# Hybrid layers with a folded q norm, column groups and paired gated v products, and combine columns fetched during the experts stage

## The chip, the core and the metric

The kernel runs on one core of a Trainium2 chip. The metric is the device time of one execution of the whole program in microseconds (us). The core's engines run their own instruction streams and meet at semaphores: PE (TensorE, matrix products), DVE (VectorE), ACT (ScalarE), POOL (GpSimd) and SP (SyncE, which here only issues transfers).

## The reference

All is float32, on a sequence of 1024 tokens of width 1024. The first block is two hybrid layers, each a chunked gated delta rule (4 heads of 128) beside chunked gated linear attention (4 heads, keys of 64, values of 128):

```python
def l2norm(x):
    return x * lax.rsqrt(jnp.sum(x * x, axis=-1, keepdims=True) + 1e-6)
def head_rms_norm(o, g):
    return o * lax.rsqrt(jnp.mean(o * o, axis=-1, keepdims=True) + 1e-6) * g

def hybrid_layer(x, w_in, conv_w, ...):
    (dn_q, dn_k, dn_v, dn_z, dn_b, dn_a, g_q, g_k, g_v, g_z, g_r) = _split(x @ w_in, IN_SIZES)
    cq, ck, cv = silu(causal_short_conv([dn_q, dn_k, dn_v], conv_w))
    q = l2norm(cq) * (DN_DK ** -0.5);  k = l2norm(ck)
    beta = sigmoid(dn_b);  g = -exp(dn_a_log) * softplus(dn_a + dn_dt_bias)
    o_dn = gated_delta_rule_chunked(q, k, cv, g, beta)
    o_dn = head_rms_norm(o_dn, dn_norm_g) * silu(dn_z)
    log_f = log_sigmoid(g_r @ gla_gate_w2 + gla_gate_b) / 16
    o_gla = gla_chunked(g_q * (64 ** -0.5), g_k, g_v, log_f)
    o_gla = head_rms_norm(o_gla, gla_norm_g) * silu(g_z)
    return layer_norm(DEEPNORM_ALPHA * x + [o_dn, o_gla] @ w_out, ln_g, ln_b)
```

The second block is two more layers, each an attention (neighbourhood, then grouped query), a route of every token to 2 of 32 experts, the experts' gated products and a combine: each token gathers its two experts' rows, mixes them by its gates and is layer-normed, with an adaptive shift and scale (the second block's modulations, sums of a bias and of products with a weight) in the first of the two.

## The kernel before

The program is a row of stages, each with a stream for every engine: inputs, constants, then for each of the two layers `hybrid_stage` (line 334) and `out_stage` (1371); then the attention and route stages; `experts_stage` (2711) and `combine_stage` (2812), both twice. In the profiled run the first hybrid stage spans about 20 to 777 us, the second 862 to 1616, the first experts stage ends near 2957 and the first combine near 3028; the last combine is the end of the program, from 4332 on.

**Hybrid stage.** It begins with a small projection (805) of 80 columns of `w_in`: beta in rows 0 to 3, a in 32 to 35, r (the gate's rank 16) in 64 to 79. Its weights' place is cleared by POOL (1085), and the load waits for that. ACT and DVE then make g and beta from 4 rows of 1024 (1327 to 1338), which are stored to `g_dram` and read back as rows for each head.

Six jobs follow: DELTA jobs 0 to 3, one head each, and GATED jobs 4 and 5, a pair of heads each. A job has a prologue (projections of 128x512 pieces, `project` 493, their eviction, for a DELTA job a convolution, Silu, the norms' squares and sums by a product with ones, `sum_squares` 502, products kk and qk, 509, and transposes, 517) and a body (the inversion by levels, 672 and 695, w and u, 703 and 707, and the scan over 8 chunks, 715 to 723; for the pairs 754 to 784). PE interleaves by hand: while it runs a body it advances the next job's prologue, a generator, by a fixed number of steps at each gap; only the first prologue runs alone. What is left of the prologue runs at the end of the body, so the number of `yield`s in a prologue decides what stands at the boundary of two jobs. ACT, DVE and POOL do the same with labelled slots:

```python
GAPS = {DELTA: (4, 4, 1, 2), GATED: (5, 6, 2, 2), None: (0, 0, 0, 0)}
def advance(work, n):
    for _ in range(n):
        next(work, None)
```

The pieces of a prologue alternate between PSUM banks 6 and 7 in the order of `DELTA_PIECES` and `GATED_PIECES`; a piece waits until the piece before it in its bank has been read.

At a job's end ACT copies the last half of o (983), squares o (985), evicts z1 (846) and copies x (955); PE then starts the next levels (672), and behind the first of them sums o's squares (`norm_sums` 647). Behind DELTA job 3 the order is another: the sums come at once, and DVE's exponent and evictions of the gated pair (1170, 1265) behind them. The root of a norm is ACT's (943 to 945). For q and k, ACT takes Ln and Exp of the sums (877, 879), and DVE multiplies (1131 for k, 1134 for q, where the factor 128 ** -0.5 goes in).

Beside the pairs' bodies, and behind the last, the six modulation vectors' sums are made (`sum_mod`, 594 to 608): for each vector two column groups, a product with the bias (604) and one with ones (608), then an ACT copy and a store (915, 917).

**Combine.** SP loads four column vectors (ln_g, ln_b, shift, scale) in a pattern whose runs are single 4-byte elements (2833), waits, then loads the next stage's weights; POOL gathers rows (2851); DVE waits for the columns, scales them (2971) and then mixes (2937). The last combine has no such columns. In the experts stage SP loads each expert's weights (2735), PE multiplies them (2634, tiles of 128x32 with 256 columns), and POOL gathers the tokens (2769).

## Time and profile before

| quantity | value |
|---|---|
| median of 3 runs | 4391.09 us (4390.46 to 4391.94) |
| profiled execution, its own time | 4389.45 us |
| its span | 4387.6 us |
| mean granted TensorE clock | 0.953 |
| PE busy | 3937.8 us, 90% |
| DVE busy | 2126.6 us, 48% |
| ACT busy | 1036.6 us, 24% |
| POOL busy | 626.0 us, 14% |

The profile is one execution. A time in a row is in us from the span's start. A float32 product is recorded as two passes, so a count of matmuls is twice that of the code. Idle time ahead of an instruction stands in brackets, with what ended it ("issue" when the profile shows no releaser). The granted clock is a share of full speed, 2.4 GHz; the lower level, 1.2 GHz, is 0.50. Idle time of an engine that is not the last to arrive costs nothing.

### The profile page before, as it was taken

The page shows a single profiled execution, that of the slowest core. Times are in us where ns is not written, and L with a number is a line of the kernel's source. Part 1 is how long each engine was busy: PE and PEld are TensorE (multiplying, and loading weights), DVE is VectorE, ACT ScalarE, POOL GpSimd, SP SyncE. Part 2 cuts the span into 40 slices and gives each one's busy share as a digit, 9 for nine tenths or more (in the row PEclk, how much of TensorE's full clock was granted, in tenths as well). Part 3 has the DMA queues.
Part 4 walks back from the last instruction along what each step waited for, and adds up shares of the span by engine and source line. Part 5 has one row for each costly group of instructions (what it writes and reads, how often), then busy time and mean ns, then how long its engine had stood idle before and what let it go on. Part 6 is the DMA issues. An engine that isn't in the chain of part 4 may idle for free. (4 is left out here: it accounts for less than half of the span.)

```text
span 4387.6 us, 79942 instructions
## 1 busy us (share of the span) xinstructions
PE 3937.8 (90%) x34826; PEld 2430.8 (55%) x34826; DVE 2126.6 (48%) x3076; ACT 1036.6 (24%) x1779; POOL 626.0 (14%) x462
## 2 busy tenths in 40 slices
PE   7999999899999998999996999875999999699973
PEld 3555655445556644666544666543566665466642
DVE  4555365455554555555565222215566787422214
ACT  3333223134432221222210000003444540000002
POOL 1232011022310110000000211101221300111111
PEclk9999999999999999999997999987999999799996
DMA  3232202323331225454522999983000112699997
GB/s 106 100 113 92 72 30 82 83 83 105 103 101 30 92 71 160 77 87 72 98 97 102 393 421 410 418 360 106 15 1 15 39 57 85 235 420 418 409 422 275
DMA packets 259927, 707.72 MB, mean 161 GB/s; under 512 B 59195, under 2 KB 185091, under 8 KB 234103
## 3 DMA queue, kind: packets, MB, share of 16 engines
q1 hardware_dynamic: 245127, 657.91, 42.2%
q0 software_dynamic: 13248, 40.38, 2.5%
q8 instruction: 280, 4.59, 0.4%
q10 hardware_dynamic: 1200, 4.24, 0.3%
q14 instruction: 72, 0.59, 0.0%
HBM read 630.25 MB, written 63.82 MB: 158 GB/s over the span
## 5 line engine op out<-in xcount | busy, mean ns | idle before, releaser
L2677 DVE TENSOR_TENSOR sb_work<-sb_work,ps 128x384 f32<-128x384 f32 (+2 forms) x66 | 34.2, 519 | 715.4 <-ACT sb_work L2664 715.4
L493 PE MATMUL ps<-sb_mixT,sb_work 128*128 128x512 f32 x768 | 359.4, 604 | 9.6 <-ACT sb_x_tok L846 5.5
L493 PE MATMUL ps<-sb_xT,sb_work 128*128 128x512 f32 x768 | 357.5, 602 | 9.6 <-ACT sb_x_tok L846 5.5
L2664 ACT ACTIVATE sb_work<-ps 128x384 f32<-128x384 f32 (+2 forms) x66 | 30.4, 461 | 1047.3 <-PE ps L2634 1047.3
L1634 PE MATMUL ps<-sb_xT,sb_work 128*128 128x512 f32 x512 | 236.2, 599 | 0.0
L2634 PE MATMUL ps<-sb_work,sb_mixT 128*32 128x256 f32 x3264 | 192.0, 398 | 41.9 <-DMA sb_work<-moe_w_up 32.4
L2634 PE MATMUL ps<-sb_work,sb_xT 128*32 128x256 f32 x3264 | 190.4, 395 | 39.7 <-DMA sb_work<-moe_w_up 30.1
L493 PEld LDWEIGHTS ps<-sb_mixT,sb_work 128*128 128x128 f32 x768 | 138.0, 192 | 147.8 <-issue 129.9
L493 PEld LDWEIGHTS ps<-sb_xT,sb_work 128*128 128x128 f32 x768 | 137.4, 191 | 147.0 <-issue 129.1
L2121 DVE TENSOR_REDUCE sb_cols<-ps 128x1 f32<-128x1024 f32 x128 | 150.7, 1219 | 85.6 <-PE ps L1964 85.5
L2634 PEld LDWEIGHTS ps<-sb_work,sb_mixT 128*32 128x32 f32 x3264 | 126.9, 115 | 106.5 <-issue 49.7
L2634 PEld LDWEIGHTS ps<-sb_work,sb_xT 128*32 128x32 f32 x3264 | 125.5, 114 | 103.9 <-issue 46.0
L2634 PE MATMUL ps<-sb_mixT,sb_xT 128*32 128x256 f32 x2496 | 146.0, 395 | 25.6 <-DMA sb_mixT<-moe_w_up 25.6
L2634 PE MATMUL ps<-sb_xT,sb_mixT 128*32 128x256 f32 x2496 | 143.8, 391 | 22.6 <-DMA sb_xT<-moe_w_up 22.6
L1940 PE MATMUL ps<-sb_work,sb_mixT 128*128 128x384 f32 x448 | 154.5, 491 | 4.1 <-PEq L93 4.1
L1634 PEld LDWEIGHTS ps<-sb_xT,sb_work 128*128 128x128 f32 x512 | 91.0, 190 | 104.2 <-issue 104.2
L2045 ACT ACTIVATE sb_work<-ps,sb_cols 128x1024 f32<-128x1024 f32 x128 | 142.7, 1115 | 17.6 <-DVE sb_cols L2121 12.1
L1974 PEld LDWEIGHTS ps<-sb_const,sb_work 128*128 128x128 f32 x1024 | 110.3, 141 | 63.3 <-issue 32.9
L1974 PE MATMUL ps<-sb_const,sb_work 128*128 128x128 f32 x1024 | 141.8, 281 | 1.9 <-DVE sb_work L2129 0.9
L2769 POOL DMA_INDIRECT sb_xT<-scratch_h,sb_slots x87 | 84.6, 973 | 400.8 <-DVE sb_xT L2672 379.5
L2769 POOL DMA_INDIRECT sb_mixT<-scratch_h,sb_slots x87 | 84.6, 972 | 400.5 <-DVE sb_mixT L2672 379.5
L2647 PE MATMUL ps<-sb_work 128*32 128x256 f32 x2496 | 141.3, 379 | 0.0
(486 smaller groups left out, 7276.1 us busy)
## 6 DMA issues: line engine op xcount, KB each, us to landing
sb_work<-moe_w_gate SPq DMA_DIRECT2D x34, 2048.0 KB, 15.2
sb_work<-moe_w_up SPq DMA_DIRECT2D x34, 2048.0 KB, 19.7
sb_work<-moe_w_down SPq DMA_DIRECT2D x32, 2048.0 KB, 22.0
sb_mixT<-moe_w_down SPq DMA_DIRECT2D x17, 2048.0 KB
sb_xT<-moe_w_down SPq DMA_DIRECT2D x17, 2048.0 KB
sb_xT<-moe_w_gate SPq DMA_DIRECT2D x16, 2048.0 KB, 16.9
sb_xT<-moe_w_up SPq DMA_DIRECT2D x16, 2048.0 KB, 21.5
sb_mixT<-moe_w_gate SPq DMA_DIRECT2D x16, 2048.0 KB, 17.1
```

Source lines behind the costliest of these rows:

```text
L493: last = pe.matmul(m.ps[:, bank, :], b.w[i][:, k, :], m.xT[:, k, half * HALF:(half + 1) * HALF], start=(k == 0), stop=(k == NK - 1))
L1634: last = pe.matmul(m.ps[:, bank, :], w[j // 2][:, k, :], m.xT[:, k, j % 2 * HALF:(j % 2 + 1) * HALF], start=(k == 0), stop=(k == NK - 1))
L1940: last = pe.matmul(m.ps[:, bank, 0:WIDE], m.xT[:, k, n * P:(n + 1) * P], w[:, k, :], start=(k == 0), stop=(k == NK - 1))
L1974: last = pe.transpose(m.ps[:, 4 + half, b * P:(b + 1) * P], prob[i % 2][head][:, half * HALF + b * P:half * HALF + (b + 1) * P], ident(m))
L2045: act.activation(prob[i % 2][head], banks(m, 2 * head), ACT.Exp, bias=top[:, column(i, head)], accum_out=total[:, column(i, head)]).then_i ...
L2121: dve.tensor_reduce(top[:, column(i, head)], banks(m, 2 * head), AX.X, ALU.max, negate=True).then_inc(found, 1)
L2634: last = pe.matmul(strip_sums(2 + 2 * (n % 2), tile[j])[:, g, :], b.x_turned[n % 2][:, g, k, :], b.gate_up[n % 2][:, :, k, j * P:(j + 1) * ...
L2647: last = pe.matmul(strip_sums(y_bank(n), tile[j])[:, g, :], b.act_turned[n % 2][:, g, k, :], b.down[n % 2][:, k, j * 2 * P:(j + 1) * 2 * P ...
L2664: act.activation(b.act[n % 2][:, 0:strips[n], :], strip_sums(2 + 2 * (n % 2))[:, 0:strips[n], 0:P], ACT.Silu).then_inc(silued, 1)
L2677: dve.tensor_tensor(act, act, strip_sums(2 + 2 * (n % 2))[:, 0:strips[n], P:2 * P], ALU.mult).then_inc(multiplied, 1)
L2769: pool.indirect_dma_start(b.x[n % 2][:, g, :], None, token_quarters(m), bass.IndirectOffsetOnAxis(m.slots[:, g, at:at + 1], 0)).then_inc(g ...
```

## The change

- **Small projection.** The sequence is cut into four quarters of 256, each the output of one column group: a tile of 32 columns of weights (r in rows 0 to 15, then beta and a, twice, from `ROW_BETA` on), four of them side by side in one bank. The operations on rows work on 256 columns at the rows of all groups. The memset goes; a_log and dt_bias come in eight small loads issued by ACT; r is copied in four pieces and g stored in four.
- **q norm folded.** The norm of o divides out a factor of q, so q is no longer normed: q's sums, roots and multiplication go. What is left of it is the epsilon: ACT squares q with scale 0.128 (in the middle of the body), DVE adds that to o's squares (`finish_squares`, at the start of the next body), and PE's norm sums wait for the addition. DVE's slots move up, and the prologue has 26 steps for 28.
- **Paired v.** The gated v projections of a pair take 256 columns of weights at once, in four pieces v0 to v3 of two token tiles each.
- **Modulation sums.** `sum_mods` makes two vectors at once in four column groups, three times; one copy and one store each.
- **Combine columns.** Their four loads move to the start of the experts stage, to a place of their own (`cols2`); the combine stage's waits for them go, and its first load is the next stage's weights.

```diff
-                ("sum_k0", 7), ("sum_k1", 7), ("sum_q0", 7), ("sum_q1", 7), ("kk0", 7), ("kk1", 7),
+                ("sum_k0", 7), ("sum_k1", 7), ("kk0", 7), ("kk1", 7),
                 ("v_tok0", 7), ("v_tok1", 7), ("k_tok0", 7), ("k_tok1", 7), ("qk0", 7), ("qk1", 7))
 GATED_PIECES = (("gate0", 6), ("gate1", 7), ("k0", 6), ("k1", 7), ("q0", 6), ("q1", 7), ("zA0", 6), ("zA1", 7),
-                ("zB0", 6), ("zB1", 7), ("vA0", 6), ("vA1", 7), ("vB0", 6), ("vB1", 7))
+                ("zB0", 6), ("zB1", 7), ("v0", 6), ("v1", 7), ("v2", 6), ("v3", 7))
...
-    b.root_k, b.root_q = b.raw[0], b.raw[1]
+    b.root_k, b.q_square = b.raw[0], m.spare[:, D:2 * D]
...
+    b.g_v_pair = m.x_tok[:, 6:8, :], m.work[:, 16 * SEQ:18 * SEQ].rearrange("p (h n) -> p h n", h=2)
+    b.w_v = m.work[:, 7 * SEQ:11 * SEQ].rearrange("p (h k n) -> p h k n", h=2, n=P)[:, :, 0:NK, :]
...
-DVE_SLOTS = {DELTA: {3: "k", 5: "q", "u": "v", "b1": "norm_k", "a2": "norm_q", "a3": "kk0", "a4": "kk1", "b4": "v_tok0",
-                     "a5": "v_tok1", "a6": "k_tok0", "b6": "k_tok1", "a7": "qk0", "end": "qk1"},
+DVE_SLOTS = {DELTA: {3: "k", 5: "q", "u": "v", "b1": "norm_k", "a2": "decay_q", "b2": "kk0", "a3": "kk1", "a4": "v_tok0",
+                     "b4": "v_tok1", "a5": "k_tok0", "a6": "k_tok1", "b6": "qk0", "a7": "qk1"},
...
-            sp.wait_ge(cleared, 1)
-            for at, column, n in ((0, C_BETA, 4), (32, C_A, 4), (64, C_GR, RANK)):
+            for at, column, n in ((0, C_GR, RANK), (ROW_BETA, C_BETA, 8), (ROW_BETA + 8, C_BETA, 8)):
...
+            sp.wait_ge(act_small, 2)
+            for j in range(4):
+                sp.dma_start(m.rows[64:64 + RANK, j * QUARTER:(j + 1) * QUARTER], b.r_rows[32 * j:32 * j + RANK, :]).then_inc(
+                    rows_stored, 16)
             sp.wait_ge(dve_small, 3)
-            sp.dma_start(g_dram[0:4, :], m.rows[32:36, :]).then_inc(rows_stored, 16)
-            sp.dma_start(g_dram[4:8, :], m.rows[0:4, :]).then_inc(rows_stored, 16)
-            sp.wait_ge(rows_stored, 32)
+            for j in range(4):
+                sp.dma_start(g_dram[:, j * QUARTER:(j + 1) * QUARTER], b.rows[32 * j + ROW_BETA:32 * j + ROW_A + DN_HEADS, :]).then_inc(
+                    rows_stored, 16)
+            sp.wait_ge(rows_stored, 128)
             load_rows(0)
...
-                sum_squares(job, "k", b.root_k, 0, 2 * job + 1)
+                sum_squares(job, "k", b.root_k, 0, job + 1)
                 yield
                 next(gate)
                 yield
-                sum_squares(job, "k", b.root_k, 1, 2 * job + 1)
+                sum_squares(job, "k", b.root_k, 1, job + 1)
                 yield
-                next(gate)
-                yield
-                sum_squares(job, "q", b.root_q, 0, 2 * job + 2)
-                yield
-                next(gate)
-                yield
-                sum_squares(job, "q", b.root_q, 1, 2 * job + 2)
-                yield
-                for _ in range(5):
+                for _ in range(7):
...
-                for i, name in ((4, "vA"), (5, "vB")):
-                    for half in range(2):
-                        bank = take_bank(job, f"{name}{half}")
-                        if half == 0:
+                for n in range(4):
+                    bank = take_bank(job, f"v{n}")
+                    if n == 0:
+                        for i in (4, 5):
                             pe.wait_ge(w_loaded[i], 16 * (pair + 1))
-                        for n in range(4 * NK):
-                            t, k = half * 4 + n // NK, n % NK
-                            last = pe.matmul(m.ps[:, bank, n // NK * P:(n // NK + 1) * P], m.xT[:, k, t * P:(t + 1) * P],
-                                             b.w[i][:, k, :], start=(k == 0), stop=(k == NK - 1))
-                            if n == 4 * NK - 1:
+                    for t in (2 * n, 2 * n + 1):
+                        for k in range(NK):
+                            last = pe.matmul(m.ps[:, bank, t % 2 * 2 * P:(t % 2 + 1) * 2 * P], m.xT[:, k, t * P:(t + 1) * P],
+                                             b.w_v[:, :, k, :], start=(k == 0), stop=(k == NK - 1))
+                            if t % 2 == 1 and k == NK - 1:
                                 last.then_inc(filled[bank], 1)
-                            if n % 4 == 3:
+                            if k % 2 == 1:
                                 yield
...
+                def sum_mods(pair):
+                    bank = 6 + pair % 2
+                    outs = [m.ps[32 * n:32 * n + 1, bank, :] for n in range(4)]
+                    if pair < 2:
+                        wait_freed(pe, len(JOBS) - 1, f"v{2 + pair}")
                     else:
-                        pe.wait_ge(part_copied, 2 * len(part_of) - 5 + v)
-                    for half in range(2):
-                        pe.matmul(outs[half], ident(m, N_MODS)[:, v:v + 1], halves(b.mod_bias)[half],
+                        pe.wait_ge(part_copied, 2 * len(part_of) - 1)
+                    for n in range(4):
+                        pe.matmul(outs[n], ident(m, N_MODS)[:, 2 * pair + n // 2:2 * pair + n // 2 + 1], halves(b.mod_bias)[n % 2],
                                   start=True, stop=False)
-                    pe.wait_ge(w_loaded[v], 16 * ((len(JOBS) if v < 4 else GLA_HEADS // 2) + 1))
-                    for half in range(2):
-                        last = pe.matmul(outs[half], ones(m)[:, 0:1], halves(b.mod_w[v])[half], start=False, stop=True)
+                    for v in (2 * pair, 2 * pair + 1):
+                        pe.wait_ge(w_loaded[v], 16 * ((len(JOBS) if v < 4 else GLA_HEADS // 2) + 1))
+                    for n in range(4):
+                        last = pe.matmul(outs[n], ones(m)[:, 0:1], halves(b.mod_w[2 * pair + n // 2])[n % 2], start=False, stop=True)
                     last.then_inc(mod_summed, 1)
...
-            for half in range(2):
-                for k in range(NK):
-                    last = pe.matmul(m.ps[0:80, half, :], b.small_w[:, k, :], m.xT[:, k, half * HALF:(half + 1) * HALF],
-                                     start=(k == 0), stop=(k == NK - 1))
+            for k in range(NK):
+                for j in range(4):
+                    last = pe.matmul(m.ps[32 * j:32 * j + 32, 0, 0:QUARTER], b.small_w[:, k, :],
+                                     m.xT[:, k, j * QUARTER:(j + 1) * QUARTER], start=(k == 0), stop=(k == NK - 1))
...
-                for n, (x, r) in enumerate(((b.kT, b.root_k), (b.qT, b.root_q))):
-                    act.wait_ge(silued, 3 * j + n + 1)
-                    act.activation(r, x, ACT.Square).then_inc(squared, 1)
+                act.wait_ge(silued, 3 * j + 1)
+                act.activation(b.root_k, b.kT, ACT.Square).then_inc(squared, 1)
...
-                for n, (name, r) in enumerate((("sum_k", b.root_k), ("sum_q", b.root_q))):
-                    for half in range(2):
-                        src, free = wait_filled(act, j, f"{name}{half}")
-                        act.activation(halves(r)[half], src, ACT.Ln, bias=m.eps6[:]).then_inc(free, 1)
-                    wait_freed(act, j, f"{name}1")
-                    act.activation(r, r, ACT.Exp, scale=-0.5).then_inc(rooted, 1)
+                for half in range(2):
+                    src, free = wait_filled(act, j, f"sum_k{half}")
+                    act.activation(halves(b.root_k)[half], src, ACT.Ln, bias=m.eps6[:]).then_inc(free, 1)
+                wait_freed(act, j, "sum_k1")
+                act.activation(b.root_k, b.root_k, ACT.Exp, scale=-0.5).then_inc(rooted, 1)
...
+                    if n == 2:
+                        if j:
+                            act.wait_ge(o_squared, norms_before[j])
+                        act.activation(b.q_square, b.qT, ACT.Square, scale=1e-3 * DN_DK).then_inc(q_squared, 1)
...
-                act.activation(b.root, b.oT, ACT.Square).then_inc(o_squared, 1)
+                act.activation(b.root, b.oT, ACT.Square).then_inc(o_half_squared, 1)
...
+            for j in range(4):
+                at = slice(32 * j + ROW_A, 32 * j + ROW_A + DN_HEADS)
+                act.dma_start(m.dt_bias[at, :], a["dn_dt_bias"][l].unsqueeze(1)).then_inc(a_loaded, 16)
+                act.dma_start(m.a_log[at, :], a["dn_a_log"][l].unsqueeze(1)).then_inc(a_loaded, 16)
...
-                dve.wait_ge(rooted, 2 * j + 1)
+                dve.wait_ge(rooted, j + 1)
                 dve.tensor_tensor(b.kT, b.kT, b.root_k, ALU.mult).then_inc(normed, 1)
                 yield "norm_k"
-                dve.wait_ge(rooted, 2 * j + 2)
-                dve.scalar_tensor_tensor(b.qT, b.qT, DN_DK ** -0.5, b.root_q, ALU.mult, ALU.mult).then_inc(normed, 1)
-                dve.wait_ge(normed, 2 * j + 2)
+                dve.wait_ge(silued, 3 * j + 2)
                 dve.wait_ge(decayed, 3 * (j + 1))
                 dve.tensor_tensor(b.qg[par], b.qT, b.G_row, ALU.mult)
-                yield "norm_q"
+                yield "decay_q"
...
+            def finish_squares(job):
+
+                if job < DN_HEADS:
+                    dve.wait_ge(q_squared, job + 1)
+                    dve.wait_ge(o_half_squared, job + 1)
+                    dve.tensor_tensor(b.root, b.root, b.q_square, ALU.add).then_inc(o_squared, 1)
...
+                if j:
+                    finish_squares(j - 1)
...
+                finish_squares(j - 1)
...
-            pool.memset(b.small_w, 0.0).then_inc(cleared, 1)
...
+            for n, src in enumerate(columns):
+                sp.dma_start(m.cols2[:, 8 * n:8 * n + 8], src.rearrange("(k p) -> p k", p=P),
+                             allow_slow_non_contiguous=True).then_inc(s["loaded_e"], 16)
...
-            if columns is not None:
-                for dst, src in zip((ln_g, ln_b, shift, scale), columns):
-                    sp.dma_start(dst, src.rearrange("(k p) -> p k", p=P), allow_slow_non_contiguous=True).then_inc(
-                        columns_loaded, 16)
+            if out is None:
                 load_group_weights(sp, first_weights, group_buffers(m).w, 0, first_loaded)
-                sp.wait_ge(columns_loaded, 64)
...
-            if columns is not None:
-                dve.wait_ge(columns_loaded, 64)
+            if out is None:
```

## Rows read from the trace of the kernel before

**Rows 1.** The page's first part: busy us, share of the span, instructions of each engine.
```profile
PE 3937.8 (90%) x34826; PEld 2430.8 (55%) x34826; DVE 2126.6 (48%) x3076; ACT 1036.6 (24%) x1779; POOL 626.0 (14%) x462
```
**Rows 2.** Windows: from:to, us, busy us (instructions) by engine, granted clock, DMA share, GB/s.
```profile
165.00:265.00 100.00, 94.97 (x653) 56.70 (x653) 59.28 (x65) 41.19 (x55) 29.98 (x14) 1.00 0.28 94
687.00:698.00 11.00, 10.80 (x49) 3.84 (x50) 9.50 (x11) 2.83 (x5) 4.72 (x2) 0.53 0.54 219
2412.00:2430.00 18.00, 18.00 (x340) 10.04 (x336) 5.38 (x6) 0.49 (x1) 7.34 (x8) 1.00 0.73 266
```
**Rows 3.** Timeline: start, duration, engine, line, out<-in, count, [idle before <-releaser]; layer 0, small projection.
```profile
30.36 13.93 PE L805 MATMUL ps<-sb_xT,sb_work 128*80 128x512 f32 x32 [0.72 <-DVE sb_xT L1322]
44.22 0.26 PE L809 MATMUL ps<-sb_const,sb_work 52*128 52x52 f32 x1
```
**Rows 4.** The same view, layer 1, small projection.
```profile
862.35 0.63 POOL L1085 MEMSET sb_work<- 128x640 f32 x1 [134.82 <-POOLq L93]
867.07 16.11 PE L805 MATMUL ps<-sb_mixT,sb_work 128*80 128x512 f32 x32 [6.47 <-DMA sb_work<-w_in]
```
**Rows 5.** The same view, a piece of the first experts stage.
```profile
2419.56 10.53 PE L2634 MATMUL ps<-sb_xT,sb_mixT 128*32 128x256 f32 x192
```
**Rows 6.** The same view, the first delta head's prologue, layer 0.
```profile
91.40 1.13 PE L502 MATMUL ps<-sb_x_tok,sb_const 128*128 128x512 f32 x2
100.56 1.13 PE L493 MATMUL ps<-sb_xT,sb_work 128*128 128x512 f32 x2 [0.95 <-ACT sb_work L846]
```
**Rows 7.** The same view, inside head 0's body, layer 0.
```profile
181.84 1.12 PE L502 MATMUL ps<-sb_x_tok,sb_const 128*128 128x512 f32 x2 [1.21 <-ACT sb_x_tok L846]
186.52 0.28 DVE L1243 TENSOR_TENSOR sb_work<-sb_work,ps 128x128 f32<-128x128 f32 x1
```
**Rows 8.** The same view, from head 0 to head 1.
```profile
214.27 1.06 ACT L985 ACTIVATE sb_mixT<-sb_mixT 128x1024 f32<-128x1024 f32 x1
216.28 1.01 ACT L955 COPY sb_work<-ps 128x1024 f32<-128x1024 f32 x1 [0.28 <-PE ps L655]
217.39 1.15 PE L672 MATMUL ps<-sb_work 64*64 64x64 f32 x32 [1.15 <-issue]
```
**Rows 9.** The same view, from head 3 to the first gated pair.
```profile
547.36 1.06 ACT L985 ACTIVATE sb_mixT<-sb_mixT 128x1024 f32<-128x1024 f32 x1
548.47 1.98 PE L647 MATMUL ps<-sb_mixT,sb_const 128*128 128x512 f32 x4
552.64 1.61 DVE L1170 TENSOR_SCALAR sb_x_tok<-ps,sb_conv 128x512 f32<-128x512 f32 x2 [1.19 <-PE ps L573]
```
**Rows 10.** The same view, the gated pairs' v projections.
```profile
540.07 1.95 PE L586 MATMUL ps<-sb_work,sb_xT 128*128 128x128 f32 x16
633.40 3.74 PE L586 MATMUL ps<-sb_work,sb_xT 128*128 128x128 f32 x32
```
**Rows 11.** The same view, the gated pairs' bodies and the end of the stage.
```profile
575.09 1.98 PE L493 MATMUL ps<-sb_xT,sb_work 128*128 128x512 f32 x4 [2.49 <-ACT sb_work L846]
687.20 1.87 PE L604 MATMUL ps<-sb_rows,sb_const 6*1 6x512 f32 x4 [2.76 <-ACT sb_work L915]
696.52 1.35 DVE L1280 COPY_PREDICATED sb_work<-sb_const,ps 128x512 f32<-128x512 int32 x2 [1.45 <-PE ps L754]
757.38 1.02 PE L604 MATMUL ps<-sb_rows,sb_const 6*1 6x512 f32 x4
758.33 1.03 PE L608 MATMUL ps<-sb_work,sb_const 128*1 128x512 f32 x4
```
**Rows 12.** The same view, the first combine, then the last.
```profile
2958.58 0.94 POOL L2851 DMA_INDIRECT sb_work<-scratch_y,sb_dest  x1 [70.86 <-issue]
2974.65 0.17 DVE L2971 TENSOR_SCALAR sb_cols<-sb_cols 128x8 f32<-128x8 f32 x1 [21.93 <-DMA sb_cols<-scratch_mods]
4332.93 0.94 POOL L2851 DMA_INDIRECT sb_work<-scratch_y,sb_dest  x1 [71.80 <-issue]
4339.49 1.28 DVE L2937 SCALAR_TENSOR_TENSOR sb_x_tok<-sb_work,sb_gates,sb_x_tok 128x1024 f32<-128x1024 f32 x1 [12.22 <-DMA sb_work<-scratch_y,sb_dest]
```

199 lines of the change are left out of this document (105 added, 94 removed).

## The prediction, made before the changed kernel was timed

> **What bounds the kernel now.** I read the page's busy line first: TensorE is busy 3937.8 of 4387.6 us, the next engine (VectorE) 2126.6 [rows 1]. The share is a mean over stages, so I then read the windows. In a typical 100 us of a hybrid layer, across one whole head's body, PE is busy 94.97 us at full clock, VectorE 59.28, ScalarE 41.19, and DMA moves at 0.28 of its rate [rows 2]. So in the hybrid stage a pass taken from PE is time taken from the program, except where PE isn't the last to arrive. Those places I looked up in the timeline, one for each edit; they decide how much of the removed work comes back. The end of the first experts stage is different: there VectorE and PE both stand still for a transfer [rows 12].
>
> The sum is made against the profiled execution, whose span is 4387.6 us; its own time is 4389.45, and the median of the runs shown is 4391.09, 3.5 above the span.
>
> **A. Small projection, columns in groups.** Now 32 recorded passes of 512 columns (each f32 product is recorded as two) run from 30.36 until the next instruction at 44.22: 13.86 us [rows 3], 0.43 a pass. The change has 64 passes of a 128x32 tile with 256 columns, four tiles side by side. The nearest row is the experts' product with just this shape: 192 in 10.53 us, 0.0548 each [rows 5]. 64 x 0.0548 = 3.5, with a fixed end of 0.2 it is 3.7, so layer 0 gains 10.1. In layer 1 the block takes 16.11 against 13.93, 2.2 more for the same work: it starts after 6.47 us of idle PE [rows 4], and I put the 2.2 down to half clock at its start. The new one pays the same 2.2: 5.9, gain 10.1. The memset of 0.63 us ahead of the small weights' load goes, and with it its wait: 0.7 in layer 1, where the block waits for that very load [rows 4]; layer 0 has its transposes to do and gains nothing. The row operations that follow (on a quarter of the columns each) were hidden behind the first projections and stay so, with more room; the eight tiny loads of constants by ScalarE and the twelve small copies and stores that replace three sit there too, and the first to need the rows is a body some 60 us later. I cost them at nothing and, should a queue hold them up, at a few us. A: 20.9, bounds 0 (a pass of 256 columns would cost half of 0.43, 64 x 0.215 = 13.8) to 22.
>
> **B. The q norm folded, first head.** The q norm's sums are two blocks of two passes; in the first prologue nothing but PE's own work runs, so their 0.96 each (1.13 less the tail) [rows 6] come back whole: 1.9. The wait of 0.95 for the z eviction by ScalarE [rows 6] was ScalarE's Ln, Ln, Exp for q ahead of it: they go, 0.95. With a small rest, 3.0 a layer, 6.0. Bounds 2 and 7.
>
> **C. The q norm folded, heads 1 to 3.** Here the prologue runs between the steps of the previous head's body. PE loses 4 passes, 1.72 us, a head. The wait of 1.21 us ahead of the sums [rows 7] goes too, but what follows in that step waits for VectorE, whose convolution keeps it until 186.52, where it makes the new values [rows 7]: PE comes earlier and waits. The other half of the argument is the head's boundary. Two steps of the generator less means that the last two pieces (1.76 us of PE work) are no longer there to fill the boundary. Its start is set by ScalarE: Square of o at 214.27 for 1.06, z's eviction, the copy of x at 216.28 for 1.01, after which PE begins the levels at 217.39, having been idle for 1.15 [rows 8]. Earlier work on PE doesn't move this chain, which hangs on the last o of the scan. VectorE's new addition (q's square onto o's) is hidden: o's square is ready at 215.33, the addition of some 1.28 (the nearest row is the 128x1024 step in [rows 12]) would be done at 216.6, and nobody needs it before PE's norm sums, behind the levels that start at 217.39. ScalarE's Square of q, 1.06, goes into the middle of the body, where ScalarE is 41% busy [rows 2]. So of 1.72 + 1.21 a head I count 0.6, the part that neither VectorE nor the boundary takes back: 3.6 for six heads. Bounds 0 (all is given back) and 10.3 (6 x 1.72, all is kept).
>
> **D. The q norm folded, from head 3 to the pair.** Between the last delta head and the first gated pair the norm sums follow at once: Square of o at 547.36 for 1.06, PE's sums at 548.47 [rows 9]. Now the addition stands between them: 1.28 and a semaphore, PE 1.3 later. VectorE itself is taken: the exponent and the gated k's eviction at 552.64 [rows 9] come later by as much and a bit more, say 1.7 in all. What is queued behind the addition on VectorE is just this exponent, and the levels of the pair wait for it. Cost 1.7 a layer, 3.4. Bounds 0 and 5.
>
> **E. Paired v products.** 16 passes with 128 columns take 1.95 us and 32 take 3.74 [rows 10]: (3.74 - 1.95) / 16 = 0.112 each. A layer has two jobs of 128 products in two passes, 512 passes, 57.2 us. 256 passes of 256 columns, at half of 0.43, are 55.0. Gain 2.1 a layer, 4.2. With 4 x 0.0548 = 0.219 a pass it is 1.1 a layer; if the loads of 128-column weights hid worse than they do now it could be 3. That v's weights 4 and 5 are now both wanted at v0 costs nothing: they are loaded a job ahead. Bounds 1 and 6.
>
> **F. Modulation sums in four groups.** The last sums show four passes in 0.95 us (757.38 to 758.33), two beside each other [rows 11]; the last pair has 16, 3.8 us. Four beside each other halve it: 1.9 a layer, on the path, since nothing else is left for PE. The earlier ones lie in the pair's bodies, where PE waits 2.76 us for ScalarE's store of the sums ahead of 687.20 and VectorE is idle for 1.45 at 696.52 [rows 11]. Three evictions for six take a part of that wait: I count 1.2 a layer. 6.2 together. Bounds 3.8 and 11.4 (all passes halved, 5.7 a layer).
>
> **G. The combine's columns.** In the first combine VectorE scales the columns at 2974.65, after 21.93 us of waiting for their landing; the first gather was issued at 2958.58. In the last combine, without columns, it is issued at 4332.93 and the first mix starts at 4339.49, 6.56 later [rows 12]. So without the column wait the first mix could start at 2965.2; it now follows the scaling, 2975.2. That is 10. But in the first combine the next stage's weights load beside the gathers, so I take 7.5. Bounds 2.5 and 10. The loads now stand at the start of the experts stage on SyncE's queue, behind which the experts' weights wait. From 2412 to 2430 PE is busy for 18.00 of 18.00 us at a DMA share of 0.73 [rows 2], so there is room of nearly 5 us; I count nothing. If they aren't covered they cost up to 5.
> The trace shows these loads to be dear: four of 4 KB end 16 us after the gathers start. The Trainium skill, DMA: Bandwidth & Descriptors, Rules for kernel authors, says that a strided last dimension is lowered to one descriptor per element, which by its word is the case for each of them; by that rule the cost moves with them into the experts stage, and G would be at its lower end, 2.5 instead of 7.5, and the sum 40.
>
> **Sum.** 20.9 + 6.0 + 3.6 - 3.4 + 4.2 + 6.2 + 7.5 = 45.0. Span 4387.6 - 45.0 = 4342.6; the median 4391.1 - 45.0 = 4346.1.
>
> **Rivals.** 1: *All removed PE work counts.* 20.9 + 4 x 4 passes x 0.43 x 2 layers (13.8) + 2.4 for the waits of the first head + 4.2 + 11.4 + 7.5 = 60.2: 4331. For it: PE's 95% [rows 2]. Against it: ScalarE's chain at the boundary [rows 8] and D. 0.17.
> 2: *The clock falls at the boundaries.* With the fill gone, PE's idle time there grows from 1.15 to some 2.7 us. After 2.76 us idle at 687.20 four passes took 1.87 us, against 1.02 at 757.38, and the granted clock from 687 to 698 was 0.53: the lower level, 1.2 GHz [rows 2, 11]. After 2.49 us at 575.09 four 512-column passes took 1.98, which is full clock [rows 11]. So it is near the edge. A fall costs up to 0.47 x 11 = 5.2 us; part of what follows waits for other engines, so I take 2 at each of six boundaries, 12: 4358. 0.15.
> The Trainium skill, TensorE: Matmul & The Clock Gate, HAM oscillation, says that idle stretches between groups of matmuls throttle the engine again each time; the row at 687.20 agrees and the one at 575.09 doesn't show it.
> 3: *The combine is bound by its gathers,* or the moved loads cost what they give: G is 0, 4353. 0.07.
> 4: *Column groups don't run side by side at this place.* A and F's halving are nothing: 4346 + 20 + 6 = 4372. Against it are 192 passes at 0.0548 [rows 5]. 0.03.
> 5: *Slower.* The half clock of rival 2, held: after each of the eight boundaries (four a layer, the one of part D included) PE stays at 1.2 GHz. It decides from the point where it eats 45 us and 8.8 more, 6.7 a boundary, that is 13.5 us at half clock after each. The only stretch like it is the 11 us at 0.53 [rows 2]. 0.01.
>
> **Chances and range.** Forecast 0.57, rivals 0.17, 0.15, 0.07, 0.03, 0.01. The forecast's own range, from the bounds of C, F and G, is 4338 to 4354. To hold 8 in 10 it must reach nearly to rivals 1 and 2: 4331 to 4358. A measurement of this kernel can tell about 0.2%, 8.8 us, from no change. All cases but the last lie beyond it on the fast side; for mishaps I have not thought of I add a little: faster 0.96, same 0.02, slower 0.02.
>
> **What the new profile should show.** A: the small product's block of some 3.7 us in layer 0, under 6 in layer 1. B, C: the ones-product only for k, half as many; PE's idle time ahead of the levels up from 1.15. D: the sums of head 3 released by VectorE, some 1.3 later after Square. E: the v block of 64 at about 0.22 a pass. F: three groups of sums. G: the first combine's VectorE starting some 7 to 9 us after the first gather; the experts' first products without a new DMA wait. The windows' clock behind each boundary settles rival 2. What would make it wrong above all: C near one of its ends, or the moved column loads holding up the experts' weights.

## The result, and the profile after

The changed kernel took 4350.28 us (median of 4, 4349.7 to 4351.16) beside 4390.83 us for the kernel before (4390.46 to 4391.94): a ratio of 0.991, 95% interval 0.9898 to 0.9923, 40.5 us less. The forecast was 4346.1, 45.0 less; the range was 4331 to 4358. The profiled execution has a span of 4349.0 us for 4387.6, 38.6 less, and a mean clock of 0.951 for 0.953. The busy line of the page answers to [rows 1]:

```profile
PE 3894.6 (90%) x34318; PEld 2403.2 (55%) x34318; DVE 2108.5 (48%) x3081; ACT 1007.0 (23%) x1749; POOL 624.2 (14%) x460
```

PE is busy for 43.2 us less, with 508 passes fewer, and its share is again 90%.

The sum over the parts can be checked, since most instructions have a counterpart in both kernels. I took the start of the same instruction in both timelines, and how much earlier it is in the changed kernel. The same marks, taken on a second trace of the unedited changed kernel (after_again, below), differ by -0.7 us at the first and -1.1 at the end of the second hybrid stage, so a difference between two marks is good to some 0.4 us there, but for one thing that is told below (the clock).

| mark | before | after | earlier by |
|---|---|---|---|
| layer 0, small projection done | 44.22 | 34.85 | 9.4 |
| head 0's levels begin | 114.12 | 100.88 | 13.2 |
| norm sums of head 0, behind the first levels of head 1 | 218.47 | 205.17 | 13.3 |
| w of head 1 | 279.66 | 267.40 | 12.3 |
| norm sums of head 1 | 321.23 | 308.35 | 12.9 |
| norm sums of head 2 | 423.99 | 410.48 | 13.5 |
| w of head 3 | 504.10 | 491.25 | 12.9 |
| norm sums of head 3 | 548.47 | 536.05 | 12.4 |
| levels of the last pair | 675.18 | 661.81 | 13.4 |
| its scan | 736.54 | 722.22 | 14.3 |
| output stage | 777.44 | 762.50 | 14.9 |
| layer 1, small projection done | 883.11 | 857.03 | 26.1 |
| head 0's levels begin | 952.99 | 923.07 | 29.9 |
| w of head 3 | 1343.38 | 1313.68 | 29.7 |
| norm sums of head 3 | 1387.75 | 1358.48 | 29.3 |
| levels of the last pair | 1516.02 | 1485.83 | 30.2 |
| output stage | 1617.52 | 1586.96 | 30.6 |
| first gather of the first combine | 2958.58 | 2928.07 | 30.5 |
| its first mix | 2975.22 | 2937.95 | 37.3 |
| last combine, first mix | 4339.49 | 4301.55 | 37.9 |

Term by term, with the letters of the prediction:

| term | forecast | found | by |
|---|---|---|---|
| A, small projection | 20.9 | 20.5 | marks: 9.4, and 26.1 - 14.9 |
| B, fold, first head | 6.0 | 7.7 | marks |
| C, fold, heads 1 to 3 | 3.6 | -0.6 | marks |
| D, fold, head 3 to the pair | -3.4 | -2.6 | undo_fold |
| E, paired v | 4.2 | 3.7 | undo_pairs |
| F, modulation sums | 6.2 | 2.0 | marks |
| G, combine's columns | 7.5 | 6.8 | marks of this pair of traces |
| the rest | 0 | 1.2 | |
| all | 45.0 | 38.7 | the spans' 38.6 |

**A.** The timeline of PE, the rows that answer to [rows 3] and [rows 4] (start, duration, engine, line, out<-in, count, idle before):

```profile
31.26 3.66 PE L815 MATMUL ps<-sb_xT,sb_work 128*32 128x256 f32 x64 [0.72 <-DVE sb_xT L1351]
34.85 0.26 PE L819 MATMUL ps<-sb_const,sb_work 52*128 52x52 f32 x1
```
```profile
851.16 5.94 PE L815 MATMUL ps<-sb_mixT,sb_work 128*32 128x256 f32 x64 [5.61 <-DMA sb_work<-w_in]
857.03 0.26 PE L819 MATMUL ps<-sb_const,sb_work 52*128 52x52 f32 x1
```

The block takes 3.59 and 5.87 us until the next instruction, against 13.86 and 16.04. 64 passes with 256 columns in four groups run 0.056 apart, what the experts' row [rows 5] had given. In layer 1 the block starts behind a wait for the weights at half clock (the granted clock from 851.2 to 857.0 is 0.60), which costs 2.3 us, as it cost 2.2 before.

**C.** Waits of PE from 0 to 1640 us (engine, tile and line, what released it: us in all, times, longest us); the line of the levels is 672 before and 682 after. Before:

```profile
PE ps L672 <- issue: 6.9, 6, 1.1
PE ps L672 <- ACT sb_work L955: 2.4, 2, 1.2
...
PE ps L754 <- issue: 6.6, 5, 2.0
PE ps L754 <- DVE sb_work L1280: 2.3, 2, 1.1
```

After:

```profile
PE ps L682 <- ACT sb_work L966: 16.3, 8, 2.3
PE ps L657 <- DVE sb_mixT L1226: 1.4, 1, 1.4
...
PE ps L764 <- issue: 13.6, 10, 2.0
PE ps L764 <- DVE sb_work L1308: 6.0, 2, 3.0
PE ps L764 <- POOL sb_work L1125: 2.9, 1, 2.9
PE ps L834 <- issue: 2.4, 2, 1.2
```

The wait ahead of a body's levels was 9.3 us in eight and is 16.3: 2.3 at each of the six boundaries of two heads, where it was 1.15 (the two first heads keep their 1.2). Of the 10.3 us of q sums' passes that are gone, 7.0 came back as idle time of PE at these boundaries. Behind the first of these waits the clock was lower:

```profile
203.53 1.71 PE L682 MATMUL ps<-sb_work 64*64 64x64 f32 x32 [2.33 <-ACT sb_work L966]
205.17 3.02 PE L657 MATMUL ps<-sb_mixT,sb_const 128*128 128x512 f32 x4
```
```profile
200.00:207.00 7.00, 4.67 (x45) 3.35 (x44) 3.70 (x3) 4.19 (x6) 2.87 (x3) 0.78 0.70 228
```

The norm sums take 3.02 us; before, at full clock, they took 1.98 (as in [rows 9]). The windows' columns are those of [rows 2]: the granted clock is 0.78 in these 7 us, so a part of them ran at 1.2 GHz. From the norm sums to w of head 1, 1.0 us is lost in layer 0 and 1.4 in layer 1; a part of the fall lies ahead of the norm sums (1.71 us for the levels' products, which take 1.15 at full clock), and a trace without it, undo_combine_2 below, puts the whole at 1.6 in each layer. Behind the other four boundaries of two heads, with the same idle time, the granted clock is 1.00.

**F.** In the last pair's levels PE waits at 764 for VectorE and GpSimd (and "issue"), 22.5 us in the two layers where it was 8.9, with 5.5 more for the sums' evictions. The window of the levels, 671.60 to 736.50 before and 658.30 to 722.20 after:

```profile
671.60:736.50 64.90, 58.16 (x356) 28.41 (x355) 57.60 (x61) 23.21 (x26) 17.42 (x7) 0.89 0.31 122
```
```profile
658.30:722.20 63.90, 51.56 (x355) 27.97 (x353) 58.59 (x61) 22.06 (x24) 17.43 (x7) 0.92 0.34 133
```

PE has 6.6 us less to do, the window is 1.0 shorter, and VectorE is busy for 58.6 of 63.9 us: by its busy share this stretch is VectorE's. No run made VectorE faster here; that less work of PE is worth nothing in it is what undo_sums shows.

### The profile page after: what moved, and what is told of

Same layout as the page of the kernel before. It is cut to its first block and busy times, and to the rows that moved or that the text cites. A ratio compares the mean times of both kernels' runs of the same rounds, so it can differ in the third digit from the quotient of the medians.

```text
span 4349.0 us, 78912 instructions
## 1 busy us (share of the span) xinstructions
PE 3894.6 (90%) x34318; PEld 2403.2 (55%) x34318; DVE 2108.5 (48%) x3081; ACT 1007.0 (23%) x1749; POOL 624.2 (14%) x460
## 5 line engine op out<-in xcount | busy, mean ns | idle before, releaser
L2075 ACT ACTIVATE sb_work<-ps,sb_cols 128x1024 f32<-128x1024 f32 x128 | 142.6, 1114 | 17.8 <-DVE sb_cols L2151 12.3
## 6 DMA issues: line engine op xcount, KB each, us to landing
sb_work<-moe_w_gate SPq DMA_DIRECT2D x34, 2048.0 KB, 14.3
```

The lines of the kernel that those rows point to most:

```text
L2075: act.activation(prob[i % 2][head], banks(m, 2 * head), ACT.Exp, bias=top[:, column(i, head)], accum_out=total[:, column(i, head)]).then_i ...
```

## The experiments

In the five comparisons the kernel before took 4390.8, 4402.9, 4385.9, 4397.3 and 4388.8 us, and the traces part by up to 8 us in the first experts stage alone (551.9 to 559.7 us from its first gather of tokens to the combine's first gather), where the DMA share is 0.98. So an edit of the hybrid stages is read by the marks (within a trace, from the first mark on), and whole times are compared only between kernels of one comparison.

### Undoing one part of the change

**undo_fold**: q normed as before (its two sums, two Ln, Exp, Square, multiplication, VectorE's slots, 28 steps), `finish_squares` gone.

```diff
-                for _ in range(7):
+                next(gate)
+                yield
+                sum_squares(job, "q", b.root_q, 0, 2 * job + 2)
+                yield
+                next(gate)
+                yield
+                sum_squares(job, "q", b.root_q, 1, 2 * job + 2)
+                yield
+                for _ in range(5):
                     next(gate)
                     yield
...
-                    dve.wait_ge(o_half_squared, job + 1)
-                    dve.tensor_tensor(b.root, b.root, b.q_square, ALU.add).then_inc(o_squared, 1)
```

> The changed kernel with q normed as before: its sums, roots and multiplication back, the Square of q and the addition gone, VectorE's slots and the 28 steps as before. Theory, from the marks of both traces: the first head's prologue is worth 7.7 us, heads 1 to 3 are worth -0.6 (the passes saved are idle time at the boundaries, less the fall of the clock after the first and the late copies in head 3's levels), the boundary of head 3 costs 2.8; together 4.3: 4354.6. Rival (the prediction's terms B, C, D): 6.2, 4356.5.

Measured: 4370.2 us, ratio 0.993 (0.9913 to 0.9946). Marks, as differences from the changed kernel: the first prologue costs 3.4 us more in each layer; from there to the norm sums of head 2 it is 0.3 more in layer 0 and 0.2 in layer 1, made of 1.9 in each for the passes, less 1.6 in each for the clock (the size of that fall is taken from undo_combine_2 below); from w of head 3 to its norm sums 1.3 less in each layer. So the fold is worth 6.7 (B), 0.5 (C) and -2.6 (D), 4.6 in all. By the marks the sum at the end of layer 1 is 5.4, with a step of 1.8 in the first pair of layer 0 that isn't the fold's (see the clock below). The theory stands; the prediction's B was right, its C was not, since it left the clock out.

**undo_sums**: one modulation vector at a time, two column groups, six evictions.

```diff
-                def sum_mods(pair):
+                def sum_mod(v):
...
-                for pause, pair in ((5, 0), (3, 1)):
-                    sum_mods(pair)
-                    yield
+                for pause, first in ((4, 0), (2, 2)):
+                    for v in (first, first + 1):
+                        sum_mod(v)
+                        yield
```

> The changed kernel with the modulation sums made one vector at a time in two column groups, as before. Theory: in the levels of the last pair VectorE sets the pace, so only the last sums' share counts, 2.0 us by the differences of the two traces at the stage's marks: 4352.3. Rival (the prediction's term): 6.2 us, 4356.5.

Measured: 4362.39 us, ratio 0.9914 (0.9897 to 0.993). Marks: in the last pair's levels 0.0 in layer 0 and -0.5 in layer 1, in its scan +0.6 in both. So four of the six sums are worth nothing, and the last two 0.6 a layer, a third of the 1.9 of PE's time that they save.

**undo_pairs**: v in four pieces of 128-column products.

```diff
-                            last = pe.matmul(m.ps[:, bank, t % 2 * 2 * P:(t % 2 + 1) * 2 * P], m.xT[:, k, t * P:(t + 1) * P],
-                                             b.w_v[:, :, k, :], start=(k == 0), stop=(k == NK - 1))
+                            last = pe.matmul(m.ps[:, bank, n // NK * P:(n // NK + 1) * P], m.xT[:, k, t * P:(t + 1) * P],
+                                             b.w[i][:, k, :], start=(k == 0), stop=(k == NK - 1))
```

> The changed kernel with the v products of 128 columns, four pieces per pair of heads. Theory: 0.95 us a job from the scan's steps (3.67 to 3.55 us a step), four jobs, 3.8: 4354.1. Rival: in the first pair's jobs it is swallowed by the boundary of head 3, so only half: 4352.2.

Measured: 4366.53 us, ratio 0.9924 (0.9907 to 0.994). Marks: 0.90, 0.94, 0.90 and 0.93 us in the four jobs, 3.7. A step of the pair's scan in the changed kernel, which answers to [rows 10]:

```profile
620.98 3.62 PE L599 MATMUL ps<-sb_work,sb_xT 128*128 128x256 f32 x16
624.53 0.44 PE L785 MATMUL ps<-sb_x_tok,sb_v_tok 128*64 128x128 f32 x4
```

16 passes of 256 columns in 3.55 us to the next instruction, 0.222 each, where 32 of 128 had taken 3.67.

### The combine's columns

**undo_combine** (and **undo_combine_2**, the same code again): the four column loads back in the combine stage; **only_combine**: the kernel before with the move alone; **after_again**: the changed kernel unedited.

```diff
+            if columns is not None:
+                for dst, src in zip((ln_g, ln_b, shift, scale), columns):
+                    sp.dma_start(dst, src.rearrange("(k p) -> p k", p=P), allow_slow_non_contiguous=True).then_inc(
+                        columns_loaded, 16)
                 load_group_weights(sp, first_weights, group_buffers(m).w, 0, first_loaded)
...
-            for n, src in enumerate(columns):
-                sp.dma_start(m.cols2[:, 8 * n:8 * n + 8], src.rearrange("(k p) -> p k", p=P),
```

> The changed kernel with the four column loads back in the combine stage, waits and order of the weights' load included. Theory: the trace of the changed kernel has the first mix 6.8 us closer to the stage's start, and this is kept to the end: 4350.3 + 6.8 = 4357.1. Rival: the moved loads hold up the experts' weights and give a part back, so that undoing them costs less, 4 us or under: 4354.

Measured: 4362.25 us, ratio 0.9917 (0.99 to 0.9934), the same as undo_sums in the same comparison. Its trace, and the changed kernel's:

```profile
2931.46 0.94 POOL L2881 DMA_INDIRECT sb_work<-scratch_y,sb_dest  x1 [70.22 <-issue]
2941.12 0.17 DVE L3001 TENSOR_SCALAR sb_cols<-sb_cols 128x8 f32<-128x8 f32 x1 [15.56 <-DMA sb_cols<-scratch_mods]
2941.69 1.28 DVE L2967 SCALAR_TENSOR_TENSOR sb_x_tok<-sb_work,sb_gates,sb_x_tok 128x1024 f32<-128x1024 f32 x1
```
```profile
2928.07 0.94 POOL L2879 DMA_INDIRECT sb_work<-scratch_y,sb_dest  x1 [69.12 <-issue]
2937.95 1.28 DVE L2965 SCALAR_TENSOR_TENSOR sb_x_tok<-sb_work,sb_gates,sb_x_tok 128x1024 f32<-128x1024 f32 x1 [9.83 <-DMA sb_work<-scratch_y,sb_dest]
```

The first mix starts 10.23 us behind the first gather with the column loads, and 9.88 us without them; in the kernel before it was 16.64 [rows 12]. That called for the next three.

> The changed kernel itself, unedited, on the chip of the next two, for a base of their times and for the stretch from the first gather to the first mix. Theory (the prediction's): 9.9 us there again. Ratio to the kernel before 0.991 again.

> The same kernel as undo_combine, again, since its trace had the first mix 10.2 us behind the first gather, where the kernel before has 16.6. Theory 1: the column loads cost about 6.8 us when they stand in the combine stage, and undo_combine's trace was a lucky one: 4 to 7 us slower than after_again. Theory 2: they land before the gathered rows anyway, the gathers set the first mix, and the 16.6 us of the kernel before were that trace's own: within 2 us of after_again.

> The kernel before with the move of the four column loads alone. Theory 1: 7 us faster than the kernel before. Theory 2: within 2 us of it.

Measured, in one comparison: before 4385.86 us, only_combine 4384.04 (ratio 0.9993, 0.9984 to 1.0002), after_again 4349.35 (0.9914, 0.99 to 0.9927), undo_combine_2 4350.27 (0.9921, 0.9907 to 0.9935). The move is worth 1.8 us in the kernel before and 0.9 in the changed one, by medians; neither is clear of the scatter, and the trace of undo_combine_2 is 0.9 ahead of after_again's at the end of the second hybrid stage, where their code is the same. From first gather to first mix: 9.9 in only_combine, 9.7 in after_again, 10.4 in undo_combine_2:

```profile
2924.21 0.94 POOL L2881 DMA_INDIRECT sb_work<-scratch_y,sb_dest  x1 [70.69 <-issue]
2934.03 0.17 DVE L3001 TENSOR_SCALAR sb_cols<-sb_cols 128x8 f32<-128x8 f32 x1 [15.71 <-DMA sb_cols<-scratch_mods]
2934.60 1.28 DVE L2967 SCALAR_TENSOR_TENSOR sb_x_tok<-sb_work,sb_gates,sb_x_tok 128x1024 f32<-128x1024 f32 x1
```

The single executions say more. The 15 of the kernel before lie in two groups, eight at 4380.4 to 4385.9 and seven at 4389.8 to 4393.0. The 11 of only_combine all lie at 4380.7 to 4385.7. undo_combine_2 has four at 4347.3 to 4352.0 and one at 4358.0, undo_combine three at 4361.1 to 4362.7 and one at 4368.6. A reading that fits is that the column loads cost nearly nothing in about half of the executions and some 7 us in the others, and that the move takes those away. The execution profiled before (4389.45) shows the late landing, those of undo_combine and undo_combine_2 the early one, and they lie in the lower part of their comparisons. But it is not shown: a trace of the kernel before from the lower group was not taken, and times can part as widely without these loads in the combine (fill, which has moved them, lies at 4349.97 to 4364.76). What decides how late they land is open.

### The boundary of two heads, and the clock

**fill**: two empty steps where the q sums stood, VectorE's slots as before the change.

```diff
-                for _ in range(7):
+                for _ in range(2):
                     next(gate)
                     yield
+                    yield
+                for _ in range(5):
+                    next(gate)
+                    yield
```

> The changed kernel with two empty steps in the prologue of a delta head where the q sums' steps were (28 again, VectorE's slots as before). So two pieces of projection stand at the boundary of two heads again. Theory: PE's idle time ahead of the levels falls from 2.3 to about 1.15 us at the six boundaries between heads, the clock doesn't fall behind the first of each layer (2.5 us), and the scan with its last o ends earlier by the 1.7 us that the pieces take: 1.2 to 1.7 a boundary and 2.5, together 10 to 12 us by the marks of the hybrid stages. Rival: in the steps left empty PE waits for VectorE's new values, and nothing but the clock's 2.5 us comes back.

Measured: 4357.76 us, ratio 0.9911 (0.9895 to 0.9928). The wait ahead of the levels (686 here) is what it was before the change, 6.9 and 2.4 in all:

```profile
PE ps L537 <- DVE sb_work L1181: 9.2, 8, 1.4
PE ps L686 <- issue: 6.9, 6, 1.1
PE ps L537 <- DVE sb_work L1167: 4.6, 6, 0.8
PE ps L529 <- DVE sb_work L1181: 4.4, 8, 0.6
PE ps L735 <- DVE sb_work L1275: 4.1, 6, 0.7
PE ps L686 <- ACT sb_work L970: 2.4, 2, 1.2
```

Marks from the changed kernel's: 1.0 and 1.4 us come back between the norm sums of head 0 and w of head 1, where the clock stays at 1.00 now; at the boundaries themselves 0.8, 0.3 and 0.2 us in layer 0, 0.5, 0.3 and 0.2 in layer 1, 2.3 together. The first of each layer holds the early part of the fall, 0.6 and 0.2, so the clock is worth 3.2 and the six boundaries some 0.25 each, 1.5. Together 4.7, not 10 to 12. The rival of this experiment is nearer. In the scan, PE's waits for VectorE at 529, 537 and 735 are 22.3 us, where the changed kernel has 14.7 (at 529 and 537, and none of 735's kind): with two steps empty PE waits there for VectorE's new values and pieces, and the filled boundary has mostly moved the wait. What the q sums cost in the scan shows against undo_fold, which has the same boundary and the same slots of VectorE: from w of head 0 to w of head 1, and from there to w of head 2, fill is 0.9 us shorter each time in both layers. So taking a head's q sums out, 1.72 us of passes, is worth half of its time where the boundary stays filled, and some 0.6 us a head in the changed kernel, where it doesn't.

**halved**: Square of o and the addition in two halves, the first in the middle of the scan.

```diff
+                        act.wait_ge(o_copied, 2 * j + c // 4 + 1)
+                        act.activation(halves(b.root)[c // 4], halves(b.oT)[c // 4], ACT.Square).then_inc(o_half_squared, 1)
-                act.wait_ge(o_copied, 2 * (j + 1))
-                act.activation(b.root, b.oT, ACT.Square).then_inc(o_half_squared, 1)
...
+                    if c == 5:
+                        dve.wait_ge(q_squared, j + 1)
+                        dve.wait_ge(o_half_squared, 2 * j + 1)
+                        dve.tensor_tensor(halves(b.root)[0], halves(b.root)[0], halves(b.q_square)[0], ALU.add)
```

> The changed kernel with ScalarE's Square of o and VectorE's addition each done in two halves, the first half in the middle of the scan, as soon as the first half of o is copied. Theory: ScalarE's chain at each boundary of two heads is 0.5 us shorter (six times, 3), and from head 3 to the pair the wait of PE's sums for the addition is 1.1 us shorter (twice, 2.2): 5 us by the marks. Rival: the chain isn't ScalarE's, but hangs on the last o alone: under 1.

Measured: 4358.8 us, ratio 0.9915 (0.9899 to 0.9932). Marks: from w of head 3 to its norm sums 1.03 us less in each layer, the theory's 1.1; the wait for the addition is 0.3 (it was 1.4). The wait ahead of the levels is 13.8 us in eight, at most 1.9, for 16.3 and 2.3:

```profile
PE ps L682 <- ACT sb_work L966: 13.8, 8, 1.9
PE ps L657 <- DVE sb_mixT L1225: 0.3, 1, 0.3
```
```profile
202.76 1.43 PE L682 MATMUL ps<-sb_work 64*64 64x64 f32 x32 [1.90 <-ACT sb_work L966]
204.11 3.34 PE L657 MATMUL ps<-sb_mixT,sb_const 128*128 128x512 f32 x4
```

So ScalarE's chain does set the boundary, by 0.4 us each. But behind 1.90 us of idle time the clock fell too, at three of the six boundaries: at the first of layer 0 the norm sums take 3.34.

**square_early**: the Square of q behind the norm's roots, a level earlier.

```diff
-                    if n == 2:
-                        if j:
-                            act.wait_ge(o_squared, norms_before[j])
-                        act.activation(b.q_square, b.qT, ACT.Square, scale=1e-3 * DN_DK).then_inc(q_squared, 1)
...
+                    if n == 1:
+                        if j:
+                            act.wait_ge(o_squared, norms_before[j])
+                        act.activation(b.q_square, b.qT, ACT.Square, scale=1e-3 * DN_DK).then_inc(q_squared, 1)
```

> The changed kernel with ScalarE's Square of q right behind the norm's roots instead of ahead of the second level's copies. Theory: in head 3's levels, where k's eviction stands just ahead of it, the Square made the copies late: 0.66 us in layer 0 and 0.45 in layer 1 come back, 1.1; nothing in heads 1 and 2. Rival: the loss there has another source: 0.

Measured: 4357.5 us, ratio 0.991 (0.9893 to 0.9926). From the norm sums of head 2 to w of head 3 it is 0.2 us shorter than the changed kernel's, and so is after_again, which has no edit. My theory of the late copies falls; the Square of q costs nothing in either place. What the marks had shown in head 3's levels (0.7 and 0.5 us) is of the size by which that stretch differs between kernels that are equal in it (-0.2 in undo_pairs, 0.5 in fill, 0.9 in halved). It holds a wait of 5.5 us for ScalarE, in all kernels, behind which PE runs at a lower clock for a while (0.66 granted in the 7.1 us behind it in layer 0 of the changed kernel).

A like stretch, in the first pair's levels, shows how the clock varies behind the same wait: PE waits there for ScalarE for 2.4 to 2.5 us in every kernel, and what follows is the same code. Layer 1, changed kernel and fill:

```profile
1385.10 3.56 PE L512 MATMUL ps<-sb_mixT,sb_work 128*128 128x512 f32 x4 [2.37 <-ACT sb_work L854]
```
```profile
1379.92 1.98 PE L512 MATMUL ps<-sb_mixT,sb_work 128*128 128x512 f32 x4 [2.39 <-ACT sb_work L858]
```

Layer 0, changed kernel and fill:

```profile
562.67 1.98 PE L512 MATMUL ps<-sb_xT,sb_work 128*128 128x512 f32 x4 [2.37 <-ACT sb_work L854]
```
```profile
559.19 3.66 PE L512 MATMUL ps<-sb_xT,sb_work 128*128 128x512 f32 x4 [2.36 <-ACT sb_work L858]
```

The same four passes take 1.98 or 3.6 us behind 2.36 to 2.39 us of idle time, once in this kernel, once in that. The marks step by 1.6 to 1.8 there, up or down, in fill, halved, sums_last, best and four of the undone kernels' traces.

The boundaries of two heads show the same. The hybrid stages of undo_combine_2 are those of the changed kernel, and its wait at the first boundary of layer 0 is too, but the clock stays at 1.00:

```profile
201.89 1.15 PE L682 MATMUL ps<-sb_work 64*64 64x64 f32 x32 [2.32 <-ACT sb_work L966]
202.97 1.98 PE L657 MATMUL ps<-sb_mixT,sb_const 128*128 128x512 f32 x4
```

From head 1's levels to w of head 1 it is 1.6 us shorter than the changed kernel in both layers: that is what the fall costs. undo_combine, the very same program, has the fall at both places. Counted over all traces by the norm sums (1.98 us at full clock, 2.6 to 3.7 behind a fall), the clock fell behind 0 of 30 boundaries with 1.15 us of idle time (before, only_combine, undo_fold, fill, best), behind 3 of 6 with 1.9 (halved), and behind 15 of 48 with 2.3 (the other eight traces). Of these 15, 13 are among the 16 first boundaries of a layer, 2 among the 32 others. Why the first is hit so much oftener is open.

### The last sums

**sums_last**: one empty step ahead of them, so that they run behind the last output product.

```diff
                         yield
+                yield
                 sum_mods(2)
```

> The changed kernel with one empty step ahead of the last modulation sums, so that they run behind the last output product of the last pair instead of ahead of it. Theory: PE's wait of 1.2 us there is for ScalarE's copy of the last o; the sums (1.9 us) cover it: 1.2 a layer, 2.4. Rival: the wait is for something behind the sums: 0.

Measured: 4356.44 us, ratio 0.9908 (0.9892 to 0.9925). From the last pair's scan to its norm sums 1.25 us less in each layer, 2.5. The changed kernel, and this one:

```profile
743.06 1.03 PE L615 MATMUL ps<-sb_rows,sb_const 6*1 6x512 f32 x8
744.02 1.04 PE L620 MATMUL ps<-sb_work,sb_const 128*1 128x512 f32 x8
744.99 0.49 PE L791 MATMUL ps<-sb_work,sb_state 64*128 64x128 f32 x4
745.41 0.71 PE L794 MATMUL ps<-sb_work 128*128 128x128 f32 x4
746.16 1.07 ACT L1034 COPY sb_mixT<-ps 128x512 f32<-128x512 f32 x2 [2.41 <-PE ps L794]
747.33 3.67 PE L834 MATMUL ps<-sb_xT,sb_mixT 128*128 128x512 f32 x8 [1.21 <-issue]
```
```profile
739.75 0.49 PE L792 MATMUL ps<-sb_work,sb_state 64*128 64x128 f32 x4
740.17 0.71 PE L795 MATMUL ps<-sb_work 128*128 128x128 f32 x4
740.81 1.03 PE L615 MATMUL ps<-sb_rows,sb_const 6*1 6x512 f32 x8
741.78 1.04 PE L620 MATMUL ps<-sb_work,sb_const 128*1 128x512 f32 x8
742.75 3.70 PE L835 MATMUL ps<-sb_xT,sb_mixT 128*128 128x512 f32 x8
```

Behind the product at 745.41 PE stands still until ScalarE has copied the last o (746.16 to 747.23); the sums, placed there, cover the copy.

### Together

**best**: fill, halved and sums_last.

> The changed kernel with three of the edits together: two empty steps in the delta prologue (fill), Square of o and the addition in halves (halved), the last modulation sums one step later (sums_last). Theory, by the marks of the three: 4.8 for fill (2.5 of it the clock), 2.1 for the wait of head 3's sums, 2.5 for the last sums, and, if ScalarE's chain still sets the six boundaries, 0.4 at each: 9.4 to 11.8 us faster than the changed kernel by the marks of the hybrid stages, ratio to the kernel before 0.989. Rival: with the boundary filled, PE is no longer behind ScalarE, and the halves give nothing at the six boundaries: 9.4.

Measured: 4344.64 us (4342.4 to 4345.83), ratio 0.9901 (0.9885 to 0.9918). At the end of the second hybrid stage it is 7.4 us ahead of the changed kernel, counted from the first mark, although the chance of the clock went against it in layer 0's first pair (1.6): 9.0 without that, the rival's 9.4. At the boundaries of two heads the marks are those of fill within 0.1, so the halves help only at head 3. It is the fastest of the kernels run; its median is 4.7 below after_again's and 5.6 below that of the changed kernel's first comparison; these are other comparisons, and the intervals of the ratios overlap.

## Why the prediction was right or wrong

The time lies in the range, 4.2 us above the forecast. By the spans 6.4 of the 45.0 are missing; the median of before lies 1.4 above its profiled execution, that of after 0.5 below, which gives 1.9 back. The forecast's own range, 4338 to 4354, is narrower than the bounds of C, F and G that it names: these add up to 4332 to 4357.

- **A, the bound and its row.** Right within 0.4. Rival 4 was wrong: the column groups run side by side here. The 0.9 us by which PE starts its first block later in the changed kernel's trace is in the 9.4; in the other kernels' traces the first mark lies 0.4 to 1.9 earlier than in that one.
- **B.** Right (6.7 by undo_fold for 6.0; the 7.7 of the marks hold 1.0 of other things, the sixteen small transposes among them, which I left out).
- **C, the step that failed.** I had both halves of the argument, VectorE's wait in the scan and ScalarE's chain at the boundary [rows 7, 8], and counted 0.6 a head for what neither takes, a guess without a working. It was met, which is luck: from w of head 1 to w of head 2, where the clock stays up, the changed kernel gains 0.62 us in both layers, 3.7 in six. What was missing from the term is the fall of the clock, which the sum put at nothing and I had made a rival with a chance of 0.15 instead: 3.2 us, 1.6 at the first boundary of each layer. The other 1.1 of the miss lies in head 3's levels, behind the 5.5 us wait, where kernels with equal code differ by as much. Rival 2 was a third right: its mechanism came, 2 of 6 times, at 1.6 us each where I had 2; another trace of the same hybrid code had none.
- **D.** Right in mechanism, at 1.3 a layer for 1.7; PE's wait was 1.4, by the row at 657, and the exponent behind the addition cost nothing more.
- **E.** Right: 3.7 for 4.2, a pass at 0.222 for 0.215.
- **F, the term most off.** 6.2 forecast, 2.0 by the marks, 0.8 by undo_sums. The levels' share (1.2 a layer) was none by undo_sums: the row of VectorE's idle 1.45 us [rows 11] was one gap in a stretch in which VectorE is busy for 57.6 of 64.9 us, and the window's row would have said so. For the last sums I said "on the path, since nothing else is left for PE"; but what the path waited for was ScalarE's copy of the last o, and PE without the sums stood idle for 1.2 of the 1.9 us.
- **G.** The sum's 7.5 came out as 6.8 in the pair of traces, and that is luck: [rows 12] showed one late landing, and the later traces with the loads in place (undo_combine, undo_combine_2) don't have it. In the comparison made for it the move is worth 1 to 2 us by medians. Rival 3 (the gathers bind anyway, 0.07) is nearly right in the traces with the early landing, 0.4 to 0.7 us. The cost that I had weighed against G, the loads taking it with them into the experts stage, didn't show: between the start of that stage and the combine's first gather the changed kernel lost 0.8 us at most, which is within the scatter of that stage. The room for them was misread all the same: 18 us with a DMA share of 0.73 [rows 2] stand for a stage that has 0.98 as a whole (2407 to 2958 us), with 55 us of PE's waits for weights.
- **Slower** (rival 5) was far from deciding: 1.6 us a fall, twice.

Two errors of the same size and sign (C and F, 8.4 us together) were partly offset by B, D and the rest.

## What to carry to other kernels

Ask of each removed piece of work what the next wait behind it is, and read the busy share of every engine in that very window, not in the stage: work taken from the busiest engine was worth all of its time where it ran alone, and a half, a third or nothing where another engine's chain set the pace. Work that stands at a boundary can also keep the clock up (no fall behind 30 boundaries with 1.15 us of idle time, 15 behind 48 with 2.3), and a piece of it can be had back for nothing by placing it behind the last result instead of ahead of it. A wait for a transfer that is read from one trace should be held against the scatter of the times, and read again in a second trace, before its whole length goes into a sum.

## What the runs showed of the hardware

TensorE's clock fell behind idle stretches of 1.9 us (halved, layer 0, at 202.76), 2.3 and 2.4 us, and stayed up behind others of the same lengths with the same code around them, even in two traces of one program (undo_combine and undo_combine_2). At the boundaries of two heads it fell behind 15 of 48 stretches of 2.3 us, 3 of 6 of 1.9 and 0 of 30 of 1.15. A fall cost 1.5 to 1.8 us, by the marks. The landing of four 4 KB column loads with single-element runs, issued beside gathers, was 9.7 to 9.8 us behind the first gather in two traces and 16.1 in a third.
